# Four raw slots in the value stage, and the residual added on TensorE

## The chip, the cores and the metric

The kernel runs as one program on one core of one Trainium2 chip. The metric is the time of one launch on the device in microseconds (us). A time is the median of several launches. The profile is of one launch, and its span runs from the first to the last instruction.

## The reference, cut to what matters

The whole computation is two transformer blocks on 256 tokens of width 2048: a gated MLP and a stick-breaking attention, then a convolution with an mLSTM, and a layer of picked experts (PEER). The change lies in the last part of that layer and in the last norm. For each token 8 heads pick 16 experts each, of 16,384; each pick has a row of `u` and a row of `v`:

```
# peer_ffn, per token t, 128 picks: eid (expert), gate (softmax of the scores)
act = gelu(sum_d u[eid, d] * x[t, d])
ff[t] = sum over picks of gate * act * v[eid]          # v: (16384, 2048)
# the last lines of second_block
h = layernorm(ALPHA * h + ff, ln2_g, ln2_b)            # ALPHA = 2 ** 0.25
```

Everything is float32.

## The kernel before, in words

The 256 tokens are two tiles of 128 (`TILES = 2`), tokens on the partitions. The residual is `h`, 128 partitions x 2 tiles x 2048 columns. All the large products before the value stage run on TensorE from weights that are streamed in, rounded on ScalarE (`hi`) and completed on VectorE (`lo`), with three products for hi*hi, lo*hi and hi*lo.

The layer of experts comes in three steps. First the `u` rows are gathered, 8 KB each, by GpSimd's indirect DMAs into `ring`, and VectorE takes the dot products (L1847). Meanwhile and behind it the picks are turned into a table: for each token, one-hot matrices (VectorE, L1830 and L1834) are multiplied on TensorE (L925, `scatter`), and ScalarE stores the result as `wT` (L1215, `store_w`). `wT` holds the weight of every one of the 16,384 experts for every token, as 128 chunks of 128 experts.

Then comes the value stage, around which the change is made. It splits the 2048 columns of `v`:

- The first 1536 columns (`V_DENSE`) are done as a dense product: all 16,384 rows of `v` are streamed, in 128 chunks of 128 rows x 1536 columns (768 KB). SyncE issues the load of chunk c into `v_raw[c % 2]` (`load_v`, L476); that slot is free once VectorE has made the low part of chunk c-2 (semaphore `v_lo`). ScalarE rounds the chunk's weights (L1224, `round_w`) and then the chunk itself (L1229, `round_v`) into `v_split`, which has two slots; it waits for TensorE to have finished chunk c-2 (`v_products`). VectorE makes the low parts (`lo_v`: L1925 for the weights, L1928 for the chunk). TensorE adds 18 products of 128x128 by 128x512 per chunk into six PSUM banks, three of `half0` and three of `half1` (`multiply_v`, L941).
- The last 512 columns (`V_GATHERED`) are done by gathering: 128 picks x 2 tiles, one indirect DMA of 128 rows of 2 KB each (L574) into four slots `v_rows`, and one multiply-add on VectorE for each (`weigh`, L1911). VectorE's program alternates: one `lo_v`, two `weigh`. A gather may be issued when VectorE has used the row set four before it.

So five engines walk through 128 chunks side by side: SyncE and GpSimd issue transfers that share the 16 DMA engines, ScalarE rounds, VectorE completes and weighs, TensorE multiplies. Each engine's program is in order; the semaphores named above couple them.

Behind the last product VectorE makes `h*ALPHA + PSUM` for each tile (L1955), the statistics (L1958 and what follows), ScalarE applies scale and shift (L1262), and VectorE multiplies by the gain and adds the bias in four pieces of 1024 columns (L1970, L1971); each piece is then stored.

## Time and profile before

| | us |
|---|---|
| median of 3 runs | 3249.94 (3248.04 to 3255.05) |
| span of the profiled execution | 3249.8 |
| TensorE (PE) busy, whole span | 2416.7 (74%) |
| VectorE (DVE) busy, whole span | 2225.1 (68%) |
| ScalarE (ACT) busy, whole span | 1095.1 (34%) |
| GpSimd (POOL) busy, whole span | 824.5 (25%) |
| L941, the products of the value stage, x2304 | 548.6 busy |
| L1928, low part of a chunk of `v`, x128 | 225.0 busy |
| L1229, rounding of a chunk of `v`, x128 | 190.6 busy |
| mean granted TensorE clock, share of 2.4 GHz | 0.872 |

The page does not give the profiled execution's own launch time; its span stands 0.1 us under the median, so sums are made against 3249.8. In the timeline each row is a start time, a duration, the engine with the line and the operation, what it writes and reads, and, in brackets, how long the engine was idle before it and who ended that wait. Rows of one line that follow one another without idle time are merged, with their count behind the x. A few matmul records can be missing, so counts of merged matmuls are nearly, not always exactly, whole chunks.

### The profile page before, as it was taken

What the parts mean: (1) busy time and instruction counts of PE and PEld (TensorE: products, weight loads), DVE (VectorE), ACT (ScalarE), POOL (GpSimd) and SP (SyncE); (2) the same over time, 40 slices, a digit from 0 to 9 for tenths busy, and PEclk for the clock granted to TensorE, in tenths of its full rate; (3) what the DMA queues carried; (4) which work ended last, traced back from release to release, by engine and by line L of the source; (5) the groups of instructions that cost most, each with busy time, mean ns of one, the idle gap of its engine ahead of it and who ended that gap; (6) DMA issues with size and microseconds to landing.
All of it is one profiled execution on the core that took longest, in us unless ns stands there. A gap on an engine that the chain in (4) does not pass through costs nothing.

```text
span 3249.8 us, 32810 instructions
## 1 busy us (share of the span) xinstructions
PE 2416.7 (74%) x10945; PEld 1994.8 (61%) x10945; DVE 2225.1 (68%) x2822; ACT 1095.1 (34%) x1069; POOL 824.5 (25%) x548
## 2 busy tenths in 40 slices
PE   7999999999999998999998400001111389998996
PEld 6888888888888886888887400001111267777775
DVE  4456455555445556356656899999999987777777
ACT  4444444444445543344444100000000134343343
POOL 1000000000000000000000466676557435555553
PEclk8999999999999998899999755555555699999998
DMA  7666556556665454455564688898789548888886
GB/s 246 194 187 185 178 181 188 186 190 188 185 184 162 136 201 157 143 162 182 181 231 140 267 368 363 373 410 339 308 315 381 230 166 287 284 285 296 282 284 211
DMA packets 164690, 766.49 MB, mean 236 GB/s; under 512 B 20124, under 2 KB 20176, under 8 KB 130672
## 3 DMA queue, kind: packets, MB, share of 16 engines
q1 hardware_dynamic: 104800, 415.28, 39.9%
q0 software_dynamic: 59792, 349.90, 27.7%
q8 instruction: 62, 1.02, 0.1%
q14 instruction: 36, 0.29, 0.0%
HBM read 763.00 MB, written 2.10 MB: 235 GB/s over the span
## 4 chain that ended last, share of the span: by engine, by line
PE 54%; DVE 25%; DMA 11%; issue 6%; ACT 3%; DVEq 1%; SPq 0%; POOL 0%; POOLq 0%; ACTq 0%
PE half L600 49%; DVE ring L1847 14%; DMA v_raw<-in_peer_v 9%; DVE v_split L1928 3%; ACT v_split L1229 2%; DVE onehot_a L1834 2%; PE half L619 1%; DMA v_rows<-in_peer_v,idx 1%; DMA w_raw<-in_a_w_in 1%; DVE onehot_b L1830 1%; PE half L941 1%; PE half L796 1%; DVEq L1834 0%; PE half L668 0%; DVE left L1745 0%
## 5 line engine op out<-in xcount | busy, mean ns | idle before, releaser
L600 PE MATMUL half<-w_split,xT 128*128 128x512 f32 x7104 | 1639.4, 392 | 14.8 <-DVE xT L1296 12.2
L600 PEld LDWEIGHTS half<-w_split,xT 128*128 128x128 f32 x7104 | 1338.1, 189 | 294.4 <-issue 8.1
L1277 DVE TENSOR_TENSOR w_split<-w_raw,w_split 128x1024 fp32r<-128x1024 f32 x592 | 722.5, 1225 | 764.6 <-ACT w_split L981 763.8
L981 ACT ACTIVATE w_split<-w_raw 128x1024 fp32r<-128x1024 f32 x592 | 626.5, 1059 | 943.2 <-PE half L600 914.8
L560 POOL DMA_INDIRECT ring<-in_peer_u,idx x256 | 480.9, 1878 | 439.6 <-DVE dots L1847 186.2
L941 PE MATMUL half<-v_split,w_x 128*128 128x512 f32 x2304 | 548.6, 395 | 46.0 <-ACT v_split L1229 43.3
L1847 DVE CUSTOM_DVE_ANT_0 ring<-ring,h 128x2048 f32<-128x2048 f32 x256 | 570.0, 2285 | 5.0 <-issue 2.5
L941 PEld LDWEIGHTS half<-v_split,w_x 128*128 128x128 f32 x2304 | 428.6, 189 | 165.8 <-ACT v_split L1229 76.0
L574 POOL DMA_INDIRECT v_rows<-in_peer_v,idx x256 | 327.9, 1281 | 333.6 <-DVE v_odd L1911 209.2
L925 PE MATMUL half<-onehot_a,onehot_b 128*128 128x128 f32 x512 | 95.0, 362 | 334.8 <-DVE onehot_a L1834 334.8
L925 PEld LDWEIGHTS half<-onehot_a,onehot_b 128*128 128x128 f32 x512 | 87.9, 268 | 342.1 <-DVE onehot_a L1834 342.1
L1928 DVE TENSOR_TENSOR v_split<-v_raw,v_split 128x1536 fp32r<-128x1536 f32 x128 | 225.0, 1758 | 102.4 <-ACT v_split L1229 102.3
L1229 ACT ACTIVATE v_split<-v_raw 128x1536 fp32r<-128x1536 f32 x128 | 190.6, 1489 | 292.5 <-DMA v_raw<-in_peer_v 292.5
L498 POOL DMA_DIRECT2D row_a<-in_final_g x1 | 0.5, 531 | 1130.2 <-DVE ao L1503 1130.2
L1215 ACT ACTIVATE wT<-half 128x1024 f32 x32 | 32.8, 1024 | 395.6 <-PE half L925 395.6
L914 PE MATMUL half<-ident,wgt 128*128 128x128 f32 x2 | 0.9, 473 | 186.2 <-DVE wgt L1863 186.2
L914 PE MATMUL half<-ident,pick_keys 128*128 128x128 f32 x4 | 1.0, 353 | 184.1 <-DVE v_odd L1877 184.1
L1911 DVE SCALAR_TENSOR_TENSOR v_odd<-v_rows,wgt,v_odd 128x512 f32<-128x512 f32 x128 | 95.8, 748 | 36.2 <-DMA v_rows<-in_peer_v,idx 35.8
L914 PEld LDWEIGHTS half<-ident,wgt 128*128 128x128 f32 x2 | 0.4, 180 | 186.8 <-DVE wgt L1863 186.8
L914 PEld LDWEIGHTS half<-ident,pick_keys 128*128 128x128 f32 x4 | 0.6, 177 | 184.3 <-issue 184.3
L1911 DVE SCALAR_TENSOR_TENSOR h<-v_rows,wgt,h 128x512 f32<-128x512 f32 x128 | 95.4, 745 | 7.1 <-DMA v_rows<-in_peer_v,idx 7.1
L1196 ACT ACTIVATE gate<-gate 128x32 f32<-128x32 f32 x8 | 1.7, 225 | 264.6 <-DVE gate L1778 264.6
(287 smaller groups left out, 1201.2 us busy)
## 6 DMA issues: line engine op xcount, KB each, us to landing
w_raw<-in_a_w_in SPq DMA_DIRECT2D x192, 512.0 KB, 3.6
v_raw<-in_peer_v SPq DMA_DIRECT2D x128, 768.0 KB, 5.8
w_raw<-in_b_w_in SPq DMA_DIRECT2D x128, 512.0 KB, 3.5
w_raw<-in_w_in SPq DMA_DIRECT2D x112, 512.0 KB, 3.5
w_raw<-in_a_w_out SPq DMA_DIRECT2D x64, 512.0 KB, 3.6
w_raw<-in_b_w_out SPq DMA_DIRECT2D x32, 512.0 KB, 4.6
w_raw<-in_w_out SPq DMA_DIRECT2D x32, 512.0 KB, 4.6
w_raw<-in_peer_wq SPq DMA_DIRECT2D x32, 512.0 KB, 3.7
```

The lines of the kernel that those rows point to most:

```text
L560: nc.gpsimd.indirect_dma_start(out=ring[:, s, :], out_offset=None, in_=peer_u_2[0], in_offset=bass.IndirectOffsetOnAxis(ap=idx[:, b, s:s + ...
L574: nc.gpsimd.indirect_dma_start(out=v_rows[n % V_SLOTS][:, :], out_offset=None, in_=peer_v_2[0].rearrange("e (s d) -> (e s) d", s=V_PARTS), ...
L600: last = mm(ps[half][:, 2 * t + n, :], xt[:, xp, kk, tok], w_split[:, s, wp, n * BANK:(n + 1) * BANK], start=(k == 0 and xp == 0 and wp == ...
L925: last = mm(by_128[s][:, n, :], onehot_b[:, s, n, :], onehot_a[:, s, n, :], start=True, stop=True)
L941: ins = mm(ps[t][:, n, :], w_x[s][:, xp, 1 - t, 0, :], v_split[s][:, vp, n * BANK:(n + 1) * BANK], start=first and xp + vp == 0, stop=last ...
L981: fn(w_split[:, k % SPLIT_SLOTS, 0, :], w_raw[:, k % RAW_SLOTS, :], ACT.Copy).then_inc(hi_done, 1)
L1229: fn(v_split[s][:, 0, :], v_raw[s][:, :], ACT.Copy).then_inc(v_hi, 1)
L1277: v.tensor_tensor(w_split[:, s, 1, :], w_raw[:, k % RAW_SLOTS, :], w_split[:, s, 0, :].bitcast(F32), ALU.subtract).then_inc(split_done, 1)
L1834: ins = v.tensor_scalar(onehot_a[:, s, n, :], iota_keys[:, :], picksT[:, 0, bass.ds(token + n, 1)], picksT[:, 2, bass.ds(token + n, 1)], A ...
L1847: v.tensor_tensor_reduce(out=ring[:, s, :], in0=ring[:, s, :], in1=h[:, t, :], scale=1.0, scalar=0.0, op0=ALU.mult, op1=ALU.add, accum_out ...
L1911: v.scalar_tensor_tensor(out=acc, in0=v_rows[m % V_SLOTS][:, :], scalar=wgt[:, bass.ds(i * BODY + m, 1)], in1=acc, op0=ALU.mult, op1=ALU.a ...
L1928: v.tensor_tensor(v_split[s][:, 1, :], v_raw[s][:, :], v_split[s][:, 0, :].bitcast(F32), ALU.subtract)\
```

## The change

`v_raw` gets four slots instead of two. The two new ones lie in the memory of `h`, over its first 1536 columns (`H` for tile 0, `H + D * 4` for tile 1). For that the dense part of `h` must be gone from there: it is put into the PSUM sums before the first chunk, as the product of a scaled identity (`ident_alpha` = ALPHA on the diagonal, made by ScalarE) with `h`, six plain float32 matmuls of 128x128 by 128x512 (`seed_h`), which open the six sums. The loads into the two new slots wait for these matmuls (`h_seeded`). ScalarE's and SyncE's loops have four chunks in a body instead of two. In the last norm the multiply-add of `h` and PSUM goes; statistics and ScalarE's scale and shift read PSUM directly, ScalarE in three instructions for each tile instead of two.

```
...
@@ -211,6 +212,7 @@
         moments = tiny("moments", [P, TILES, 2])
         shift = tiny("shift", [P, TILES])
         warm = tiny("warm", [P, 1])
+        ident_alpha = sb("ident_alpha", [P, P], F32, SCR + 48 * KB)
 
 
         xg = sb("xg", [P, TILES, D], F32, SCR)
@@ -313,7 +315,8 @@
         V_CHUNK = V_DENSE * 4
         lists = packer(ROWS, LISTS)
         v_raw = [lists("v_raw0", [P, V_DENSE]),
-                 sb("v_raw1", [P, V_DENSE], F32, ROWS + 24 * KB - 288 - V_CHUNK)]
+                 sb("v_raw1", [P, V_DENSE], F32, ROWS + 24 * KB - 288 - V_CHUNK),
+                 sb("v_raw2", [P, V_DENSE], F32, H), sb("v_raw3", [P, V_DENSE], F32, H + D * 4)]
         w_x = [lists(f"w_x{n}", [P, 2, TILES, 1, P], F32R) for n in range(2)]
         v_split = [sb("v_split0", [P, 2, V_DENSE], F32R, RAW), sb("v_split1", [P, 2, V_DENSE], F32R, SCR + 32 * KB)]
         v_rows = ([sb(f"v_rows{n}", [P, V_GATHERED], F32, RAW + 2 * V_CHUNK + n * V_GATHERED * 4) for n in range(2)]
@@ -388,7 +391,9 @@
-        v_raw_landed = [sem("v_raw_landed0"), sem("v_raw_landed1")]
+        v_raw_landed = [sem(f"v_raw_landed{n}") for n in range(V_RAW_SLOTS)]
+        alpha_ready = sem("alpha_ready")
+        h_seeded = sem("h_seeded")
@@ -471,17 +476,19 @@
                 if s == 1 and isinstance(c, int):
 
                     sp.wait_ge(scattered, TOKENS // SCATTER + 2)
+                if s == 2 and isinstance(c, int):
+                    sp.wait_ge(h_seeded, 1)
                 if not isinstance(c, int):
-                    sp.wait_ge(v_lo, c - 1)
+                    sp.wait_ge(v_lo, c - (V_RAW_SLOTS - 1))
                 sp.dma_start(v_raw[s][:, :], peer_v_2[0, bass.ds(c * N_KEYS, N_KEYS), 0:V_DENSE])\
                     .then_inc(v_raw_landed[s], 16)
 
             sp.wait_ge(keys_known, TILES)
-            for s in range(2):
+            for s in range(V_RAW_SLOTS):
                 load_v(s, s)
-            with sp.Fori(1, N_KEYS // 2) as i:
-                for s in range(2):
-                    load_v(i * 2 + s, s)
+            with sp.Fori(1, N_KEYS // V_RAW_SLOTS) as i:
+                for s in range(V_RAW_SLOTS):
+                    load_v(i * V_RAW_SLOTS + s, s)
             for n in range(2 * TILES):
                 t, b = divmod(n, 2)
                 cols_ = slice(b * COLS, (b + 1) * COLS)
@@ -934,12 +941,21 @@
                 turn_picks(f"wgtT{t}", [wgt[:, t * PICKS:(t + 1) * PICKS]])
                 scatter(t)
 
-            def multiply_v(c, s, first=False, last=False):
+            def seed_h():
+
+                pe.wait_ge(alpha_ready, 1)
+                for t in range(TILES):
+                    for n in range(V_BANKS):
+                        ins = mm(ps[t][:, n, :], ident_alpha[:, :], h[:, t, n * BANK:(n + 1) * BANK], start=True,
+                                 stop=False)
+                ins.then_inc(h_seeded, 1)
+
+            def multiply_v(c, s, last=False):
 
                 def one(t, xp, vp):
                     for n in range(V_BANKS):
                         ins = mm(ps[t][:, n, :], w_x[s][:, xp, 1 - t, 0, :], v_split[s][:, vp, n * BANK:(n + 1) * BANK],
-                                 start=first and xp + vp == 0, stop=last and vp == 1)
+                                 start=False, stop=last and vp == 1)
                     return ins
 
                 pe.wait_ge(v_hi, c + 1)
@@ -956,9 +972,8 @@
 
             pe.wait_ge(w_stored, TOKENS // SCATTER + 2)
             emptied("wgtT1")()
-            multiply_v(0, 0, first=True)
-            multiply_v(1, 1)
-            with pe.Fori(1, N_KEYS // 2 - 1) as i:
+            seed_h()
+            with pe.Fori(0, N_KEYS // 2 - 1) as i:
                 for s in range(2):
                     multiply_v(i * 2 + s, s)
             multiply_v(N_KEYS - 2, 0)
@@ -1219,17 +1234,18 @@
 
             def round_w(c, s):
 
-                if not isinstance(c, int):
+                if not (isinstance(c, int) and c < 2):
                     act.wait_ge(v_products, c - 1)
-                fn(w_x[s][:, 0, :, :, :], wT[:, :, bass.ds(c, 1), :], ACT.Copy).then_inc(w_hi, 1)
+                fn(w_x[s % 2][:, 0, :, :, :], wT[:, :, bass.ds(c, 1), :], ACT.Copy).then_inc(w_hi, 1)
 
             def round_v(c, s):
 
-                act.wait_ge(v_raw_landed[s], c * 8 + (16 - 8 * s))
-                fn(v_split[s][:, 0, :], v_raw[s][:, :], ACT.Copy).then_inc(v_hi, 1)
+                act.wait_ge(v_raw_landed[s], c * (16 // V_RAW_SLOTS) + (16 - 16 // V_RAW_SLOTS * s))
+                fn(v_split[s % 2][:, 0, :], v_raw[s][:, :], ACT.Copy).then_inc(v_hi, 1)
 
             for n in range(TILE_GROUPS + 1):
                 gate_exponent(n)
+            fn(ident_alpha[:, :], ident[:, :], ACT.Copy, scale=ALPHA).then_inc(alpha_ready, 1)
             pick_gelu(0)
             picks_out("pkT0", picksT[:, 0:2, 0:P], 2)
             picks_out("wgtT0", picksT[:, 2:3, 0:P], 1)
@@ -1248,18 +1264,22 @@
             for s in range(2):
                 round_w(s, s)
             round_v(1, 1)
-            with act.Fori(1, N_KEYS // 2) as i:
-                for s in range(2):
-                    round_w(i * 2 + s, s)
-                    round_v(i * 2 + s, s)
+            for s in range(2, V_RAW_SLOTS):
+                round_w(s, s)
+                round_v(s, s)
+            with act.Fori(1, N_KEYS // V_RAW_SLOTS) as i:
+                for s in range(V_RAW_SLOTS):
+                    round_w(i * V_RAW_SLOTS + s, s)
+                    round_v(i * V_RAW_SLOTS + s, s)
 
             warm_root()
             for t in range(TILES):
                 root_next(slice(t, t + 1))
                 act.wait_ge(shift_ready, t + 1)
-                for b in range(2):
-                    cut = h[:, t, b * COLS:(b + 1) * COLS]
-                    fn(cut, cut, ACT.Identity, bias=shift[:, t:t + 1], scale=rstd[:, t:t + 1]).then_inc(normed, 1)
+                affine = dict(bias=shift[:, t:t + 1], scale=rstd[:, t:t + 1])
+                fn(h[:, t, 0:COLS], flat[t][:, 0:COLS], ACT.Identity, **affine).then_inc(normed, 1)
+                fn(h[:, t, COLS:V_DENSE], flat[t][:, COLS:V_DENSE], ACT.Identity, **affine)
+                fn(h[:, t, V_DENSE:], h[:, t, V_DENSE:], ACT.Identity, **affine).then_inc(normed, 1)
 
 
         @block.vector
@@ -1919,13 +1939,16 @@
                 dve.wait_ge(v_used, (t + 1) * PICKS + V_SLOTS)
                 step(v.tensor_tensor(h[:, t, V_DENSE:], h[:, t, V_DENSE:], v_odd[:, :], ALU.add))
 
-            def lo_v(c, s):
+            def lo_v(c, n):
+
+                s = n % 2
 
                 dve.wait_ge(w_hi, c + 1)
                 v.tensor_tensor(w_x[s][:, 1, :, :, :], wT[:, :, bass.ds(c, 1), :], w_x[s][:, 0, :, :, :].bitcast(F32),
                                 ALU.subtract).then_inc(w_lo, 1)
                 dve.wait_ge(v_hi, c + 1)
-                v.tensor_tensor(v_split[s][:, 1, :], v_raw[s][:, :], v_split[s][:, 0, :].bitcast(F32), ALU.subtract)\
+                v.tensor_tensor(v_split[s][:, 1, :], v_raw[n % V_RAW_SLOTS][:, :], v_split[s][:, 0, :].bitcast(F32),
+                                ALU.subtract)\
                     .then_inc(v_lo, 1)
 
             with dve.Fori(0, P // SCATTER // 2) as i:
@@ -1951,11 +1974,8 @@
                 v.bn_stats(bn[:, t, V_BANKS, :], h[:, t, V_DENSE:])
             dve.wait_ge(v_products, N_KEYS)
             for t in range(TILES):
-                dst = h[:, t, 0:V_DENSE]
-                step(v.scalar_tensor_tensor(out=dst, in0=dst, scalar=ALPHA, in1=flat[t][:, 0:V_DENSE], op0=ALU.mult,
-                                            op1=ALU.add))
                 for n in range(V_BANKS):
-                    ins = v.bn_stats(bn[:, t, n, :], h[:, t, n * BANK:(n + 1) * BANK])
+                    ins = v.bn_stats(bn[:, t, n, :], flat[t][:, n * BANK:(n + 1) * BANK])
                 step(ins)
                 step(tile_moments(t))
                 v.tensor_scalar(meansq[:, t:t + 1], moments[:, t, 1:2], LN_EPS, None, ALU.add).then_inc(stat, 1)
```

SyncE's program at the start of the value stage, before (`v_raw_155` and `v_raw_156` are the two slots; a row in brackets names the semaphores waited for):

```order
L476 DMA v_raw_155<-in_peer_v 128x1536 [waits keys_known]
L476 DMA v_raw_156<-in_peer_v 128x1536 [waits scattered]
L482 UNCONDITIONAL_BRANCH
L482 ISA
L476 ISA [waits v_lo]
L476 DMA v_raw_155<-in_peer_v 128x1536
L476 ISA [waits v_lo]
L476 DMA v_raw_156<-in_peer_v 128x1536
```

and after (four slots, `v_raw_156` to `v_raw_159`):

```order
L483 DMA v_raw_156<-in_peer_v 128x1536 [waits keys_known]
L483 DMA v_raw_157<-in_peer_v 128x1536 [waits scattered]
L483 DMA v_raw_158<-in_peer_v 128x1536 [waits h_seeded]
L483 DMA v_raw_159<-in_peer_v 128x1536
L489 UNCONDITIONAL_BRANCH
L489 ISA
L483 ISA [waits v_lo]
L483 DMA v_raw_156<-in_peer_v 128x1536
L482 REGISTER_ALU
L483 ISA [waits v_lo]
L483 DMA v_raw_157<-in_peer_v 128x1536
L482 REGISTER_ALU
```

The load of chunk 2 moved from behind the first `v_lo` to behind `h_seeded`, and each later load waits for the low part of four chunks before.

TensorE's program between the last one-hot product and the second group of products of the first chunk, before:

```order
L925 MATMUL half<-onehot_a,onehot_b 128x128 [waits w_stored,onehot_done]
L925 MATMUL half<-onehot_a,onehot_b 128x128 x7
L919 REGISTER_ALU
L919 COMPARE_AND_BRANCH
L941 MATMUL half<-v_split_159,w_x_157 128x512 [waits v_hi,w_hi,half_free_a,w_stored]
L941 MATMUL half<-v_split_159,w_x_157 128x512 x5
L941 MATMUL half<-v_split_159,w_x_157 128x512 [waits w_lo]
```

and after (L949 is `seed_h`):

```order
L932 MATMUL half<-onehot_a,onehot_b 128x128 [waits w_stored,onehot_done]
L932 MATMUL half<-onehot_a,onehot_b 128x128 x7
L926 REGISTER_ALU
L926 COMPARE_AND_BRANCH
L949 MATMUL half<-h,ident_alpha 128x512 [waits alpha_ready,half_free_a,w_stored]
L949 MATMUL half<-h,ident_alpha 128x512 x5
L976 UNCONDITIONAL_BRANCH
L976 ISA
L957 MATMUL half<-v_split_162,w_x_160 128x512 [waits w_hi,v_hi]
L957 MATMUL half<-v_split_162,w_x_160 128x512 x5
L957 MATMUL half<-v_split_162,w_x_160 128x512 [waits w_lo]
```

Six matmuls stand ahead of the first chunk, and the first chunk's products are now in the loop.

VectorE's program behind the last row set (`half` is PSUM), before:

```order
L1920 TENSOR_TENSOR h<-h,v_odd 128x512 [waits v_used]
L1951 BN_STATS bn<-h 128x6 [waits dve_step]
L1951 BN_STATS bn<-h 128x6
L1955 SCALAR_TENSOR_TENSOR h<-h,half 128x1536 [waits v_products]
L1958 BN_STATS bn<-h 128x6 [waits dve_step]
L1958 BN_STATS bn<-h 128x6 x2
L1335 BN_AGGR moments<-bn 128x2 [waits dve_step]
L1961 TENSOR_SCALAR meansq<-moments 128x1 [waits dve_step]
L1317 RECIPROCAL rstd<-root 128x1 [waits rooted]
L1963 SCALAR_TENSOR_TENSOR shift<-moments,rstd 128x1 [waits dve_step]
L1955 SCALAR_TENSOR_TENSOR h<-h,half 128x1536
L1958 BN_STATS bn<-h 128x6 [waits dve_step]
```

and after:

```order
L1940 TENSOR_TENSOR h<-h,v_odd 128x512 [waits v_used]
L1974 BN_STATS bn<-h 128x6 [waits dve_step]
L1974 BN_STATS bn<-h 128x6
L1978 BN_STATS bn<-half 128x6 [waits v_products]
L1978 BN_STATS bn<-half 128x6 x2
L1355 BN_AGGR moments<-bn 128x2 [waits dve_step]
L1981 TENSOR_SCALAR meansq<-moments 128x1 [waits dve_step]
L1337 RECIPROCAL rstd<-root 128x1 [waits rooted]
L1983 SCALAR_TENSOR_TENSOR shift<-moments,rstd 128x1 [waits dve_step]
L1978 BN_STATS bn<-half 128x6 x3
```

L1955 is gone for both tiles, and the statistics read `half`; the rows behind them are unchanged.

## Rows read from the trace of the kernel before

**Rows 1.** The page's chain of waits over the whole span, shares by engine and line.
```profile
PE 54%; DVE 25%; DMA 11%; issue 6%; ACT 3%; DVEq 1%; SPq 0%; POOL 0%; POOLq 0%; ACTq 0%
```

**Rows 2.** The chain of waits from 2550 us on, shares by line.
```profile
by line: DMA v_raw<-in_peer_v 43.3%; DVE v_split L1928 12.9%; ACT v_split L1229 10.7%; issue 8.4%; DMA v_rows<-in_peer_v,idx 5.7%; DVE onehot_a L1834 3.8%; PE half L941 2.6%; DVE ring L1847 2.6%; DVE h L1911 1.2%; DVEq L1834 1.0%; PE half L
```

**Rows 3.** TensorE's timeline in the value stage: first run, a long one, longest idle, last.
```profile
2634.16 12.58 PE L941 MATMUL half<-v_split,w_x 128*128 128x512 f32 x54 [1.75 <-ACT w_x L1224]
...
2688.81 20.72 PE L941 MATMUL half<-v_split,w_x 128*128 128x512 f32 x90 [0.40 <-ACT v_split L1229]
...
2932.17 22.30 PE L941 MATMUL half<-v_split,w_x 128*128 128x512 f32 x90 [4.80 <-ACT v_split L1229]
...
3200.60 26.45 PE L941 MATMUL half<-v_split,w_x 128*128 128x512 f32 x108 [1.90 <-ACT v_split L1229]
```

**Rows 4.** Waits from 2600 us on: who waited for whom; total us, times, longest.
```profile
ACT v_split L1229 <- DMA v_raw<-in_peer_v: 292.5, 125, 7.3
POOL v_rows L574 <- DVE v_odd L1911: 209.2, 93, 71.7
...
DVE v_odd L1911 <- DMA v_rows<-in_peer_v,idx: 35.8, 44, 1.9
```

**Rows 5.** The instructions on tile v_raw: durations ns min/median/max, then landing.
```profile
L1229 ACT ACTIVATE v_split<-v_raw x128: 1471/1490/1497, 2577.8 to 3221.1; 128x1536 fp32r<-128x1536 f32 x128
L1928 DVE TENSOR_TENSOR v_split<-v_raw,v_split x128: 1748/1758/1809, 2634.5 to 3222.7; 128x1536 fp32r<-128x1536 f32 x128
...
DMA to landing us min/median/max: 4.0/5.8/10.2
```

**Rows 6.** DMA queues, 2640 to 3220 us: packets, MB, share of the 16 engines; issues.
```profile
q1 hardware_dynamic: 18002, 98.29, 50.6%
q0 software_dynamic: 20322, 67.79, 33.0%
...
row_b<-in_ln_b POOLq DMA_DIRECT2D x1, 1024.0 KB, 11.8
```

**Rows 7.** Windows: us, busy (count) of PE, PEld, DVE, ACT, POOL, PEclk, DMA share, GB/s.
```profile
2600.00:2634.00 34.00, 21.05 (x165) 18.95 (x164) 30.30 (x88) 11.66 (x13) 0.00 (x0) 1.00 0.01 2
2640.00:3220.00 580.00, 535.72 (x2250) 418.42 (x2249) 434.16 (x534) 231.88 (x250) 319.64 (x253) 0.99 0.84 286
```

**Rows 8.** Timeline of one gather's round, and landings of all v_rows gathers.
```profile
2961.14 0.74 DVE L1911 SCALAR_TENSOR_TENSOR v_odd<-v_rows,wgt,v_odd 128x512 f32<-128x512 f32 x1
...
2963.35 1.91 POOL L574 DMA_INDIRECT v_rows<-in_peer_v,idx  x1 [0.31 <-issue]
...
2970.72 0.75 DVE L1911 SCALAR_TENSOR_TENSOR v_odd<-v_rows,wgt,v_odd 128x512 f32<-128x512 f32 x1 [1.09 <-DMA v_rows<-in_peer_v,idx]
...
DMA to landing us min/median/max: 3.4/5.2/11.7
```

**Rows 9.** Timeline: VectorE from one chunk to the next without a wait.
```profile
2654.94 0.42 DVE L1925 TENSOR_TENSOR w_x<-wT,w_x 128x256 fp32r<-128x256 f32 x1
...
2658.27 0.42 DVE L1925 TENSOR_TENSOR w_x<-wT,w_x 128x256 fp32r<-128x256 f32 x1
```

**Rows 10.** Timeline at the stage's start; float32 matmuls of 256 columns by form.
```profile
2632.55 1.02 ACT L1215 ACTIVATE wT<-half 128x1024 f32 x1 [2.17 <-PE half L925]
...
L668 PE MATMUL half<-gv,wsT 128*128 128x256 f32 x64 | 14.5, 379 | 0.0
```

**Rows 11.** Timeline of the last norm.
```profile
3227.70 1.74 DVE L1955 SCALAR_TENSOR_TENSOR h<-h,half 128x1536 f32<-128x1536 f32 x1
3229.47 1.88 DVE L1958 BATCH_NORM_STATS2 bn<-h 128x6 f32<-128x512 f32 x3
...
3237.08 1.23 DVE L1970 TENSOR_TENSOR h<-h,row_g 128x1024 f32<-128x1024 f32 x1
3237.19 2.37 ACT L1262 ACTIVATE h<-h,shift,rstd 128x1024 f32<-128x1024 f32 x2 [0.42 <-DVE shift L1963]
```

More of the change, by code:

```diff
@@ L71 @@
 V_SLOTS = 4
+V_RAW_SLOTS = 4
 SCATTER = 8
@@ L1938, in stream_v @@
                     for n in range(BODY // 2):
-                        lo_v(i * (BODY // 2) + (t * (N_KEYS // TILES) + n), n % 2)
+                        lo_v(i * (BODY // 2) + (t * (N_KEYS // TILES) + n), n)
                         weigh(t, i, t * PICKS + 2 * n)
```

## The prediction

> **What bounds the kernel now.** I read the page's chain of waits first, since it says which engine the end hangs on: 54% of the span is TensorE [rows 1], nearly all of it in stages that the change does not touch. The same chain cut to the last 700 us reads quite otherwise: the transfer of a raw chunk leads with 43.3%, VectorE's low part has 12.9%, ScalarE's rounding 10.7%, and the products only 2.6% [rows 2]. So the value stage is not bound by TensorE, though TensorE looks full in it.
>
> TensorE's timeline gives the stage's size. It runs from 2634.16 to 3200.60 + 26.45 = 3227.05, which is 592.9 us for 128 chunks, 4.63 us per chunk. Where it is fed it does five chunks in 20.72 us, less the 0.16 us by which the last record outlasts its issue (estimate: a record lasts 0.39, the next starts after 0.23), so 4.11 us per chunk; I use 4.12 [rows 3]. All 128 at this rate take 527.4 us, so 65.5 us of the stage are gaps, each ended by ScalarE's rounding of a chunk. The waits say what ScalarE stood for: 292.5 us in 125 waits for the transfer of a raw chunk [rows 4].
>
> The reason is a loop with two slots. A load is issued at the end of the low part of two chunks before; it lands after 5.8 us (median), is rounded in 1.49 and gets its low part in 1.76 [rows 5]. That is 9.05 us for two chunks, 4.53 each, and with some 0.2 us of hand-overs 4.63, the measured pace. So the loop, not an engine, sets it. The other bounds, per chunk:
>
> - TensorE 4.12.
> - DMA engines: 83.6% of 580 us busy, 485 us for 125 chunks, 3.88 us [rows 6]. Their rate is 286 GB/s at a share of 0.84 [rows 7], so some 340 if full; at 4.12 us per chunk the share would be 0.94.
> - VectorE 3.33 where it does not wait: from 2654.94 to 2658.27 [rows 9].
> - The gathers' loop, with four slots, so two chunks for a round: multiply-add 0.74, then 1.47 until the gather is issued (2961.88 to 2963.35, the one ahead of it in GpSimd's queue included), then the wait for the rows. Here the rows were used 7.37 us after the issue, and VectorE waited for them: a round of 9.58, 4.79 per chunk. With the median landing of 5.2 the round is 7.4, 3.7 per chunk [rows 8]. With L for the latency, the pace is (2.21 + L) / 2. GpSimd itself has room: it waits 209.2 us for VectorE to free a slot [rows 4].
>
> **The change part by part.** *Four raw slots.* The load of chunk c+4 is issued at the low part of chunk c. The loop of 9.26 us is now shared by four chunks, 2.3 us each, far below 4.12. The stall of raw chunks goes, and TensorE is next at 4.12, with the gathers between 3.7 and 4.8 close beside it. VectorE now waits for gathers 35.8 us in 44 waits, 0.8 us each [rows 4]. It has 4.12 - 3.33 = 0.79 us to spare per chunk, and its low part may come late, since only the last third of a chunk's products waits for it; most single waits are swallowed. But the DMA engines go from 0.84 to above 0.9, and L with them; TensorE keeps pace only while L stays under 2 x 4.12 - 2.21 = 6.03, and the landings spread from 3.4 to 11.7. Bounds for the stage: 527.4 us if nothing reaches TensorE, and (2.21 + 7.37) / 2 x 128 = 613 us if every gather were as late as the one shown. I take 545, nearer the first, since L's median of 5.2 is well under 6.03: 527.4, plus 15 us (0.12 per chunk) for late gathers, plus 3 of the present 4.8 us gap before 2932.17 [rows 3], where two 1 MB rows stand ahead of gathers in GpSimd's queue (11.8 us to land [rows 6]); slots of raw chunks bridge only the dense half of this. Gain 47.9 us. All loads keep their number and size, and SyncE passes only waits for the low part, so nothing is queued behind a later wait than before.
>
> By the Trainium skill, "DMA: Bandwidth & Descriptors", section "Queues, rings and completion order", each DMA engine takes turns between the queues with work, one packet each. No row shows a standing backlog, because two slots can't build one.
>
> *Residual first, through the identity.* Six float32 matmuls of 512 columns are new at the stage's start. The nearest rows are float32 matmuls of 256 columns, two records for each, 64 records in 14.5 us, 0.227 a record [rows 10]. At twice the width 0.44 to 0.45, so 12 x 0.44 = 5.3 us; bounds 12 x 0.23 = 2.8 (as cheap as the stage's own products) and 10.6 (half clock; but the clock is 1.00 from 2600 to 2634 [rows 7]). They start when the last table part is stored, 2632.55 + 1.02 = 2633.57 [rows 10], while the first product now starts at 2634.16, after ScalarE's rounding, which now runs beside them. Cost 5.3 - 0.6 = 4.7 us, all on the path, since TensorE is what the stage waits for. The loads of chunks 2 and 3 wait for this: issued at 2638.9 instead of 2636.3. They land by 2644.7, are rounded by 2646.3, and TensorE wants chunk 2 at 2638.9 + 8.2 = 2647.1; covered by 0.8 us, and if the load takes as long as the 10.2 us maximum it costs 3.6 us once. Scaling the identity is one short ScalarE instruction long before, hidden by VectorE's picks; uncovered it would cost under its 1.02 us row for eight times the columns. The first low part and its gathers are not behind the seeds and may run ahead.
>
> *Last norm.* Two multiply-adds of 1.74 go from VectorE's path, 3.5 us; VectorE is never idle for long from 3227.70 to the end [rows 11]. They also started 0.65 us after the last product, since VectorE had the last row set to finish; with TensorE the pacer it should be done sooner, and I count 0.6 us. The six statistics read PSUM. L1955 read PSUM and took 1.74 [rows 11], where L1928 took 1.758 on as many columns of SBUF [rows 5]: no surcharge, cost nothing; the bound on the other side is 1 us in all (estimate: 10% of 2 x 1.88, rounded up for hand-overs). ScalarE's third instruction for each tile adds some 0.2 us; VectorE's eight passes of 1.23 start at 3237.08 while ScalarE's two for the same tile took 2.37 together, so it is covered; if not, 0.4 us. In all -4.1.
>
> The Trainium skill, "VectorE: DVE Perf Modes", section "The TRN2 errata", gives VectorE a fixed 120 cycles with a PSUM source against 58 with SBUF. By it the six statistics would lose 6 x 65 ns = 0.4 us; the rows above do not bear it out.
>
> Sum: 3249.8 - 47.9 + 4.7 - 4.1 = 3202.5 us. The median is 0.1 above the span, so **3203 us**.
>
> **The rivals.**
>
> A, *TensorE alone paces.* Late gathers are all swallowed: 527.4 for the stage, 3249.8 - 65.5 + 0.6 = 3185 us. For it: at 2688.81 five chunks ran with no gap even now. Against it: five runs on a stretch need not hold for 128, and the 4.8 us gap has a cause that stays.
>
> B, *gathers take the place of the raw loads.* Mean L of 6.7, midway between the median and the late ones: 4.45 per chunk, 570 us, -23 + 0.6, so 3227 us. For it: VectorE is already made to wait by the second gather of a chunk 44 times, and the load on the DMA engines grows. Against it: the issue pattern per chunk stays, one raw load and two gathers, so the two compete hardly more often than now. The packet rule of the Trainium skill above is a milder version of this; estimated by it, 3249.8 - 36 + 0.6 = 3214 us.
>
> C, *the slots bring nothing.* If the long landing of raw chunks is the DMA engines' own limit, more slots only lengthen the landing, and the pace stays at 4.6: 3250 us. Against it: the engines are busy 0.84, and the shortest landing is 4.0 us.
>
> D, *slower.* With up to four raw loads queued, gathers land late in every round. The point from which it decides is L = 2 x 4.63 - 2.21 = 7.05; beyond it the stage is longer than now. At L = 7.5, just over the late one shown, the pace is 4.86, the stage 622 us, and the whole 3249.8 + 29 + 0.6 = 3279 us. For it: 7.37 was seen. Against it: it would have to be the mean.
>
> **How the numbers follow.** Forecast 0.55 (its own range 3192 to 3214), A 0.15, B 0.20, C 0.04, D 0.06. No change means within 0.2% (6.5 us) of the median, about what a measurement can tell here; so faster 0.90, same 0.04, slower 0.06. The range reaches down to A and up past B: 3184 to 3232.
>
> **What would show it.** In the profile after: ScalarE's wait for raw chunks falls from 292.5 us to a few tens, and its rounding waits for TensorE's products instead; TensorE's gaps in the stage fall from 65 us to about 18, ended by low parts (VectorE) rather than by rounding; DMA share 0.9 or more at some 308 GB/s; twelve records near 0.44 us ahead of the first chunk; VectorE's statistics within 0.7 us of the last product, at 0.63 us each. The forecast fails if VectorE's waits for gathers grow beyond 100 us with a pace over 4.4 (B or D), or if raw chunks still end ScalarE's waits (C).

## The result

| | before | after |
|---|---|---|
| median, us | 3250.27 (8 runs) | 3233.53 (8 runs) |
| span of the profiled execution, us | 3249.8 | 3230.0 |
| ratio of the times | | 0.995, 95% interval 0.9939 to 0.9961 |

The kernel became faster by 0.5%, some 17 us, where 47 us were forecast; the measured time lies just above the range that was given (3232). The profiled execution is 19.8 us shorter than that of before, and the following speaks of these two. (The forecast took a median to stand 0.1 us above a profiled span. Here the profiled launch took 3232.14 us for a span of 3230.0, and the median stands 1.4 us above that, so the two can't be compared to a microsecond.) The value stage runs from 2636.96 to 3208.84, 571.9 us, 4.47 us per chunk instead of 4.63. So of the 19.8 us the stage gave 21.0; its first product came 2.8 us later, and what follows the last product was 1.5 us shorter.

TensorE's timeline after, the seeds, the first run of chunks, a run of five chunks, the two gaps beside the gain rows and the last run; the brackets tell the idle time and who ended it:

```profile
2632.11 5.42 PE L949 MATMUL half<-h,ident_alpha 128*128 128x512 f32 x12 [1.21 <-ACT wT L1230]
...
2636.96 51.61 PE L957 MATMUL half<-v_split,w_x 128*128 128x512 f32 x222
...
2716.28 21.55 PE L957 MATMUL half<-v_split,w_x 128*128 128x512 f32 x90 [0.52 <-DVE w_x L1947]
...
2922.96 4.72 PE L957 MATMUL half<-v_split,w_x 128*128 128x512 f32 x18 [2.08 <-DVE w_x L1947]
2929.85 8.80 PE L957 MATMUL half<-v_split,w_x 128*128 128x512 f32 x36 [2.17 <-DVE w_x L1947]
...
3193.28 15.56 PE L957 MATMUL half<-v_split,w_x 128*128 128x512 f32 x66 [0.52 <-DVE w_x L1947]
```

Against [rows 3] the reader sees another releaser: not ScalarE's rounding but VectorE's low part of the weights. The first 222 products go in 51.61 us, 0.232 each; VectorE starts ahead, and it takes some twelve chunks until its lateness has reached TensorE. Later 90 products take 21.55 us, where 90 took 20.72 in [rows 3]: part of the time is lost in pauses of a few tenths inside a merged run, between the three groups of a chunk. So the pace must be taken from duration and count together, not from the idle time shown in brackets.

Who waited for whom after 2640 us, after; total us, times, longest:

```profile
DVE v_odd L1931 <- DMA v_rows<-in_peer_v,idx: 123.3, 117, 2.4
...
PEld half L957 <- DVE w_x L1947: 33.1, 51, 2.6
PEld half L957 <- DVE v_split L1950: 32.2, 84, 0.5
```

and the same view from 2600 us on has one more row of interest:

```profile
ACT v_split L1244 <- DMA v_raw<-in_peer_v: 2.5, 1, 2.5
```

ScalarE's 292.5 us of waits for raw chunks [rows 4] are 2.5. VectorE's waits for the second gather of a chunk grew from 35.8 us in 44 to 123.3 in 117: nearly every chunk. The chain of waits says the same; its shares from 2640 to 3200 us, after:

```profile
by line: DMA v_rows<-in_peer_v,idx 56.1%; issue 15.6%; POOL v_rows L581 13.2%; DVE v_odd L1931 5.5%; PE half L957 4.2%; DVE v_split L1950 1.5%; DVE h L1931 0.8%; DMA v_raw<-in_peer_v 0.8%; POOLq L579 0.5%; DVEq L1931 0.5%; DVE w_x L1947 0.4
```

In [rows 2], over a longer stretch, the raw transfer led with 43.3% and the gathers had 5.7%; over the same 560 us of the trace before they have 54.2% and 6.3%. The landings of all gathers, after, against a median of 5.2 in [rows 8]:

```profile
DMA to landing us min/median/max: 3.4/6.4/11.8
```

Three rounds of second gathers in the timeline after; VectorE's use of a row set, GpSimd's gather into its slot, and the use of what it brought:

```profile
2646.66 0.75 DVE L1931 SCALAR_TENSOR_TENSOR v_odd<-v_rows,wgt,v_odd 128x512 f32<-128x512 f32 x1 [0.58 <-DMA v_rows<-in_peer_v,idx]
...
2648.53 1.70 POOL L581 DMA_INDIRECT v_rows<-in_peer_v,idx  x1 [0.30 <-issue]
...
2650.21 0.75 DVE L1931 SCALAR_TENSOR_TENSOR v_odd<-v_rows,wgt,v_odd 128x512 f32<-128x512 f32 x1
...
2652.10 2.26 POOL L581 DMA_INDIRECT v_rows<-in_peer_v,idx  x1 [0.30 <-issue]
...
2655.96 0.75 DVE L1931 SCALAR_TENSOR_TENSOR v_odd<-v_rows,wgt,v_odd 128x512 f32<-128x512 f32 x1 [1.57 <-DMA v_rows<-in_peer_v,idx]
...
2657.49 2.05 POOL L581 DMA_INDIRECT v_rows<-in_peer_v,idx  x1 [1.38 <-DVE v_odd L1931]
...
2660.07 0.80 DVE L1931 SCALAR_TENSOR_TENSOR v_odd<-v_rows,wgt,v_odd 128x512 f32<-128x512 f32 x1 [0.69 <-DMA v_rows<-in_peer_v,idx]
...
2664.40 0.75 DVE L1931 SCALAR_TENSOR_TENSOR v_odd<-v_rows,wgt,v_odd 128x512 f32<-128x512 f32 x1 [0.86 <-DMA v_rows<-in_peer_v,idx]
```

The gather issued at 2648.53 is used at 2655.96, after 7.43 us; that of 2652.10 after 7.97; that of 2657.49 after 6.91. The round from 2646.66 to 2655.96 is 9.30 us, the next of the same slots, 2655.96 to 2664.40, is 8.44: in the mean 8.87 for two chunks, 4.44 each, close to the stage's 4.47. Over all second gathers of this trace, the landing comes 7.0 us after the issue in the median; in the trace before, where only half of them (63) can be told, 5.3. That 5.3 is the middle of two groups. When GpSimd's issue of the gather took under 1.2 us, the rows landed 4.6 us after it in the mean (33 gathers); when it took 1.9 or more, 6.9 (18 gathers). And the 44 second gathers for which VectorE already waited before were used 7.1 us after their issue in the mean; after the change there are 117 such, and they were used 7.2 us after. So the late gathers did not become later, nearly all became late: the changed kernel is paced by a round that stood just under the bound before.

The windows of the two traces over the same 500 us, before and then after (columns as in [rows 7]):

```profile
2640.00:3140.00 500.00, 461.95 (x1941) 359.63 (x1940) 374.72 (x461) 199.99 (x216) 274.96 (x219) 1.00 0.84 287
```

```profile
2640.00:3140.00 500.00, 486.01 (x2014) 368.14 (x2013) 381.52 (x472) 201.28 (x224) 328.08 (x224) 1.00 0.84 298
```

The DMA engines' share stayed at 0.84, and they moved 11 GB/s more. That they were not full is shown below, by e6. GpSimd is busy 53 us longer for as good as the same number of gathers.

The tail after, from the last row set to VectorE's first pass over the normed tiles:

```profile
3208.64 0.75 DVE L1931 SCALAR_TENSOR_TENSOR v_odd<-v_rows,wgt,v_odd 128x512 f32<-128x512 f32 x1 [2.42 <-DMA v_rows<-in_peer_v,idx]
...
3211.36 1.88 DVE L1978 BATCH_NORM_STATS2 bn<-half 128x6 f32<-128x512 f32 x3
...
3214.38 1.20 ACT L1280 ACTIVATE h<-half,shift,rstd 128x1024 f32<-128x1024 f32 x1 [0.43 <-DVE shift L1983]
...
3217.35 1.22 DVE L1990 TENSOR_TENSOR h<-h,row_g 128x1024 f32<-128x1024 f32 x1
```

The three statistics from PSUM take 1.88 us, exactly what they took from SBUF [rows 11]. But VectorE reaches them 2.5 us after the last product (3208.84), because the last gather was late as well.

### The profile page after: what moved, and what is told of

Read it like the earlier page. It is cut to its first block, busy times and chain, and to the rows that moved or that the text cites. A ratio compares the mean times of both kernels' runs of the same rounds, so it can differ in the third digit from the quotient of the medians.

```text
span 3230.0 us, 32701 instructions
## 1 busy us (share of the span) xinstructions
PE 2428.1 (75%) x10957; PEld 1987.9 (62%) x10957; DVE 2219.0 (69%) x2820; ACT 1088.4 (34%) x1072; POOL 877.8 (27%) x548
## 4 chain that ended last, share of the span: by engine, by line
PE 54%; DVE 23%; DMA 11%; issue 7%; POOL 2%; ACT 1%; DVEq 1%; POOLq 0%; SPq 0%; ACTq 0%
PE half L607 49%; DVE ring L1867 14%; DMA v_rows<-in_peer_v,idx 10%; POOL v_rows L581 2%; DVE onehot_a L1854 2%; PE half L626 1%; DVE v_odd L1931 1%; PE half L957 1%; DMA w_raw<-in_a_w_in 1%; DVE onehot_b L1850 1%; PE half L803 1%; DVEq L1854 0%; PE half L675 0%; DVE left L1765 0%; PE half L906 0%
## 5 line engine op out<-in xcount | busy, mean ns | idle before, releaser
L957 PE MATMUL half<-v_split,w_x 128*128 128x512 f32 x2304 | 557.0, 397 | 14.9 <-DVE w_x L1947 13.9
L957 PEld LDWEIGHTS half<-v_split,w_x 128*128 128x128 f32 x2304 | 421.5, 188 | 150.2 <-DVE w_x L1947 33.1
L581 POOL DMA_INDIRECT v_rows<-in_peer_v,idx x256 | 381.3, 1489 | 267.0 <-DVE v_odd L1931 159.4
L1931 DVE SCALAR_TENSOR_TENSOR v_odd<-v_rows,wgt,v_odd 128x512 f32<-128x512 f32 x128 | 96.5, 754 | 123.4 <-DMA v_rows<-in_peer_v,idx 123.3
L1239 ACT ACTIVATE w_x<-wT 128x256 fp32r (+1 forms) x128 | 53.5, 419 | 339.1 <-PE half L957 339.1
```

The lines of the kernel that those rows point to most:

```text
L581: nc.gpsimd.indirect_dma_start(out=v_rows[n % V_SLOTS][:, :], out_offset=None, in_=peer_v_2[0].rearrange("e (s d) -> (e s) d", s=V_PARTS), ...
L957: ins = mm(ps[t][:, n, :], w_x[s][:, xp, 1 - t, 0, :], v_split[s][:, vp, n * BANK:(n + 1) * BANK], start=False, stop=last and vp == 1)
L1931: v.scalar_tensor_tensor(out=acc, in0=v_rows[m % V_SLOTS][:, :], scalar=wgt[:, bass.ds(i * BODY + m, 1)], in1=acc, op0=ALU.mult, op1=ALU.a ...
```

## The experiments

Theory G, formed from the two traces: two rounds bound the stage side by side, and each spans as many transfers as it has slots. Before, the raw loads' round of two slots gave 4.63 us per chunk; after, the second gather's round of four slots (two chunks) gives 4.47. Rivals: the DMA engines have no more to give; the gain came from the seeds and the norm; VectorE's own work is the bound; the loops' register work delays gathers. Times are medians of four to ten runs (two for e2), with the ratio to the kernel before and its 95% interval; each ratio goes by runs of the kernel before taken together with the version's own, so it can differ a little from that of the medians shown. The pace is that of TensorE's stage in one traced execution. It was the fastest run of its version in e3 and e8 and the slowest in e4 (of 3199 to 3222 us), e7 and e10.

| version | median us | ratio (interval) | us per chunk |
|---|---|---|---|
| before | 3250.27 | 1 | 4.63 |
| changed | 3233.53 | 0.995 (0.9939 to 0.9961) | 4.47 |
| e1, two raw slots | 3249.78 | 0.9993 (0.9983 to 1.0003) | 4.61 |
| e2, half raw loads | 3182.95 | 0.9788 (0.9769 to 0.9808) | 4.09 |
| e3, multiply-add between | 3225.94 | 0.9922 (0.9906 to 0.9939) | 4.42 |
| e4, slots four and two | 3210.46 | 0.9861 (0.984 to 0.9881) | 4.40 |
| e5, raw loads later | 3223.16 | 0.9917 (0.9894 to 0.994) | 4.44 |
| e6, six row slots in turn | 3180.0 | 0.9786 (0.9769 to 0.9802) | 4.10 |
| e7, gain rows last | 3230.91 | 0.9936 (0.9919 to 0.9952) | 4.48 |
| e8, three raw loads ahead | 3228.52 | 0.9934 (0.9918 to 0.9951) | 4.45 |
| e9, e6 with two raw slots | 3244.43 | 0.9976 (0.9966 to 0.9986) | 4.55 |
| e10, e6 with four row slots | 3227.26 | 0.9914 (0.9898 to 0.9931) | 4.45 |
| e11, e6 with gain rows last | 3181.41 | 0.9778 (0.9761 to 0.9794) | 4.08 |

**e1: the slots undone, the rest kept.**

```
-V_RAW_SLOTS = 4
+V_RAW_SLOTS = 2
```

> The changed kernel with the raw slots back at two; the residual still goes in through the identity and the last norm still reads PSUM. Theory G (the gathers' round now paces the changed kernel at 4.47 us per chunk, and the two-slot loop of raw loads did so before at 4.63): the pace goes back to 4.63, the stage to about 593 us, so about 21 us slower than the changed kernel, near 3254 us, and TensorE's 5.0 us of seeds and the 4 us of the last norm about cancel against the kernel before. Rival (the gain came from the seeds and the norm, not from the slots): it stays near 3233 us.

The pace went back to 4.61, and against the kernel before nothing measurable is left. So the whole gain is the slots', and the seeds and the norm cancel. In its trace TensorE's stage ends 16.3 us before the end of VectorE's last pass, against 19.7 before; this stretch is called the tail in what follows.

**e2: half of the raw traffic.**

```
-sp.dma_start(v_raw[s][:, :], peer_v_2[0, bass.ds(c * N_KEYS, N_KEYS), 0:V_DENSE])\
+wide = V_DENSE if isinstance(c, int) else V_DENSE // 2
+sp.dma_start(v_raw[s][:, 0:wide], peer_v_2[0, bass.ds(c * N_KEYS, N_KEYS), 0:wide])\
     .then_inc(v_raw_landed[s], 16)
```

> The changed kernel, but each raw load after the first four brings only the first 768 of its 1536 columns; the rest of a slot is stale, so the dense part is not the reference's. All engines' work is the same, the raw traffic on the DMA engines is halved. Theory G with contention on the DMA engines as the reason for late gathers: the second gather of a chunk lands 7.0 us after its issue in the changed kernel; here under 6 us, and TensorE paces at 4.12 to 4.2 (stage 528 to 538 us). If it is GpSimd's longer issue (1.9 us instead of 0.95 beside VectorE's low part) that makes it late, the issue stays at 1.9 us, the landing near 6.5, and the pace about 4.25.

TensorE paces at 4.09, and VectorE's waits for gathers fall to 8.6 us:

```profile
DVE v_odd L1932 <- DMA v_rows<-in_peer_v,idx: 8.6, 21, 1.0
```

GpSimd's issue of second gathers stayed as long as in the changed kernel, 1.97 us in the mean against 1.89, so that alone does not make them late. What shrank is the time from the end of the issue to VectorE's use, from 5.3 to 4.1 us in the mean. The raw traffic beside them makes it long, with four row slots and everything else equal. Were it the issue alone, a pace of about 4.25 was forecast; it did not come.

**e3: the two multiply-adds apart.** `lo_v` calls the first `weigh` of the chunk between its two low parts.

```
-def lo_v(c, n):
+def lo_v(c, n, between):
...                                       # low part of the weights
+between()
 dve.wait_ge(v_hi, c + 1)
...                                       # low part of the chunk
-lo_v(i * (BODY // 2) + (t * (N_KEYS // TILES) + n), n)
-weigh(t, i, t * PICKS + 2 * n)
+lo_v(i * (BODY // 2) + (t * (N_KEYS // TILES) + n), n,
+     lambda: weigh(t, i, t * PICKS + 2 * n))
 weigh(t, i, t * PICKS + 2 * n + 1)
```

> The changed kernel with VectorE's order in a chunk changed: low part of the weights, first multiply-add, low part of the chunk, second multiply-add. The two slots of a chunk come free 1.8 us apart or more instead of 0.66, so the second gather is not queued behind the first in GpSimd's program or on the DMA engines. Theory G: its round shrinks from 8.94 us to about 8.2, the pace to 4.15, 35 to 40 us faster than the changed kernel, near 3195 us. Rival (VectorE's lateness, not the gathers, holds TensorE): the low part of the chunk comes 0.75 us later than now and the kernel gets no faster or a few us slower.

Faster than the changed kernel by some 8 us, not 35 to 40: a miss of G's size. Now the first gather is the late one:

```profile
DVE h L1931 <- DMA v_rows<-in_peer_v,idx: 108.5, 106, 4.2
...
DVE v_odd L1931 <- DMA v_rows<-in_peer_v,idx: 13.3, 10, 2.1
```

The lateness moved with the order. Whatever gather is issued while VectorE makes the 1.75 us low part takes GpSimd longer: in the changed kernel the issue of second gathers took 1.94 us in the mean when it overlapped that work (120 of them) and 0.94 when not, that of first gathers 1.08; here first gathers take 1.58 and second ones 1.12.

**e4: four slots for the second gather, two for the first.**

```
+ROW_SLOT = [0, 1, 2, 3, 0, 4, 2, 5]      # by pick % 8; slots 4 and 5 lie behind v_split1
...
+for m in range(BODY, 2 * BODY, 2):       # the second gather of a chunk, two chunks further ahead
+    gather_row(i, m)
+    gather_row(i, m + 5)
...
```

> The changed kernel with six slots for gathered rows instead of four: the second gather of each chunk has four slots and is issued four chunks ahead, the first keeps two. Theory G: the second gather's round spans four chunks and no longer binds, the first one's is 0.75 + 0.8 + 5.5 = 7.1 us for two chunks; TensorE paces at 4.12 to 4.2, near 3195 us, and VectorE's 129 us of waits for gathers nearly go. Rival (the DMA engines give no more than 296 GB/s in this mix of rows and chunks): landings get longer in turn, the pace stays near 4.45, 3230 us.

Half of it came true. The second gather never waits, but the first, still two chunks ahead, now makes VectorE wait 121.7 us in 71 waits. Its round had been hidden behind the other's. The times lie between the forecast and the rival's 3230, from 3199 to 3222 us.

**e5: raw loads 1.4 us later.**

```
-sp.wait_ge(v_lo, c - (V_RAW_SLOTS - 1))
+sp.wait_ge(v_used, c * 2 - 2)
```

> The changed kernel, with each raw load issued when VectorE has used both row sets of the chunk four before (v_used) instead of at that chunk's low part: 1.4 us later against the gathers, same depth. Raw chunks land 5.3 us before ScalarE takes them (median in the changed kernel), so they can wait. Theory P (the second gather is late because the next raw load, issued at a fixed phase, runs beside it): its landing falls from 7.0 by 0.5 to 1 us, the pace to 4.2 to 4.35, 3205 to 3220 us. Rival B (the two transfers share the DMA engines wherever the load stands, since they are 83% busy): unchanged within 5 us, 3233.

Between the two forecasts, and with runs from 3210 to 3249 us the least steady of all. The waits split, 63.6 us for second and 54.3 us for first gathers, 118 together against 129: the phase moves the lateness more than it removes it.

**e6: six row slots in turn.** GpSimd's and VectorE's loops of the stage are written out, since 16 picks a body do not go into six slots.

```
-V_SLOTS = 4
+V_SLOTS = 6
...
+                  + [sb(f"v_rows{n}", [P, V_GATHERED], F32, SCR + 44 * KB + (n - 4) * V_GATHERED * 4) for n in (4, 5)])
...                                       # GpSimd, the slot being m % V_SLOTS
+for m in range(TILES * PICKS):
...
+    if m == 4:
+        pool.wait_ge(scattered, TOKENS // SCATTER + 2)
+    pool.wait_ge(v_used, m + 1)
...
```

> The changed kernel with six slots for gathered rows used in turn, so every gather is issued three chunks ahead of its use instead of two (GpSimd's and VectorE's loops of the value stage are written out for it). Theory G: the round of some 8.9 us now spans three chunks, 3.0 us each, and nothing of it reaches TensorE but the two gain rows: 4.12 to 4.2 per chunk, 3193 to 3203 us, and VectorE's waits for gathers under 20 us. With four and two slots (the run before) the first gather, still two chunks ahead, was the late one: 121.7 us in 71 waits. Rival (DMA engines full): pace 4.4, 3225 us.

It is 70 us faster than the kernel before and 53 faster than the changed one. TensorE's stage is two merged rows with one gap:

```profile
2635.00 267.17 PE L957 MATMUL half<-v_split,w_x 128*128 128x512 f32 x1176
2902.88 256.30 PE L957 MATMUL half<-v_split,w_x 128*128 128x512 f32 x1128 [0.71 <-DVE w_x L1947]
```

That is 524.2 us for 128 chunks, 4.095 each. The window of the same 500 us:

```profile
2640.00:3140.00 500.00, 499.29 (x2202) 412.83 (x2201) 420.68 (x522) 220.43 (x246) 394.52 (x245) 1.00 0.92 326
```

The DMA engines give 326 GB/s at a share of 0.92 where the changed kernel stood at 298 and 0.84. This rules out that they were full. VectorE's own work is not the bound either: it is busy 420.68 of these 500 us, while TensorE is busy all but 0.71. With TensorE last, VectorE starts the statistics at once and the tail is 15.7 us, against 19.7 before: the 4 us that were forecast.

**e7: gain rows last.**

```
-    if t == 0:
-        pool.wait_ge(v_products, D // P)
-        row(row_g2[:, :], ln2_g_2[0], "rows_ln2")
-        row(row_b2[:, :], ln2_b_2[0], "rows_ln2")
+pool.wait_ge(v_products, D // P)          # behind both tiles' gathers
+row(row_g2[:, :], ln2_g_2[0], "rows_ln2")
+row(row_b2[:, :], ln2_b_2[0], "rows_ln2")
```

> The changed kernel with the two 1 MB rows of gain and bias loaded behind the last gather instead of between the tiles. In the changed kernel TensorE loses some 4 us at 2921 and 2928 beside them. Theory G: 3 to 6 us faster, near 3229 us, since gathers pace all the stage and those two loads stand in their queue. Rival: the loads then end too late for the last norm (needed 14 us after the last gather) and it is 0 to 5 us slower.

2.6 us faster in the median, with overlapping runs (3229.12 to 3234.86 against 3231.48 to 3237.91); the trace, which is of the slowest of the four runs, shows none of it (4.48 per chunk). Inconclusive.

**e8: one raw load less ahead.**

```
-sp.wait_ge(v_lo, c - (V_RAW_SLOTS - 1))
+sp.wait_ge(v_lo, c - (V_RAW_SLOTS - 2))
```

> The changed kernel with each raw load held until the low part of the chunk three before, so one of the four slots is always empty: same phase against the gathers, one load less ahead. Theory P: nothing changes, 3233 us within 4, since raw chunks now land 5.3 us early and would still land 1 us early. If a standing backlog of raw loads is what makes gathers late, the second gather's landing falls under 6.5 us and the kernel gets 10 to 25 us faster.

5 us faster, at the edge of what was allowed for "nothing"; VectorE waited 118.9 us for second gathers instead of 123.3, and still used them 7.2 us after their issue in the mean. The fourth load ahead, which was to bring 10 to 25 us if it mattered, is not what makes gathers late. The run says less of the raw traffic itself: in the changed kernel a raw load is issued once per chunk, every 4.47 us, and lands 6.2 us later (median), so some 1.4 are under way in the mean, and holding one slot back leaves that rate as it is.

**e9 and e10: controls for e6.**

```
-V_RAW_SLOTS = 4                      # e9
+V_RAW_SLOTS = 2
-V_SLOTS = 6                          # e10, otherwise written out as e6
+V_SLOTS = 4
```

> Six row slots used in turn as in the fast version, but two raw slots as before the change. Theory G says that the two rounds are separate bounds, and the slower one sets the pace: the raw loads' round of two slots again gives about 4.6 us per chunk, 3245 to 3252 us, although gathers no longer make VectorE wait. Rival (row slots alone would have brought the gain, the raw slots nothing): 3180 to 3200 us.

> The fast version with four row slots instead of six, GpSimd's and VectorE's loops of the value stage still written out: a control for the writing out. Theory G: as the changed kernel, 3233 us within 5, second gathers late again. Rival (the loops' register work and branches were what delayed gathers): near 3180 us.

Both as G says. With six row slots and two raw slots ScalarE waits for raw chunks again:

```profile
ACT v_split L1244 <- DMA v_raw<-in_peer_v: 259.0, 122, 5.5
```

and with four row slots VectorE waits for gathers again, written out or not:

```profile
DVE v_odd L1929 <- DMA v_rows<-in_peer_v,idx: 122.2, 112, 2.5
```

Four raw slots alone are worth 17 us. Six row slots, with the loops written out, are worth 5 us with two raw slots (e9 against e1) and 53 with four (e6 against the changed kernel): each deepening alone runs into the other round. Writing out alone is worth some 6 us by the medians and 12 by the ratios (e10 against the changed kernel), so the loops' instructions did cost something, and why is not shown; the row slots themselves are worth 47 of the 53 us by the medians (e6 against e10), and in e9 nothing that can be told from the writing out.

**e11: e6 with gain rows last.** Moved as in e7.

> The version with six row slots, and the rows of gain and bias loaded behind the last gather. With six slots TensorE has one gap of 0.7 us in the whole stage, so there is at most that to win; the loads land about 12 us after the last gather's issue at 3147.7, at about 3161, and the norm wants them at about 3167. Theory G: the same time within 2 us, 3180.

The same time, as expected. e6 stays the fastest version that was run, with e11 beside it.

## Why the prediction was wrong, step by step

- *The raw loads' round bounds the kernel.* Right. e1 goes back to 4.61, and the wait for raw chunks fell from 292.5 to 2.5 us with four slots. Its removal was said to leave a round of 2.3 us per chunk; the raw chunks did land 5.0 us before ScalarE took them, in the median of all 128.
- *TensorE is next at 4.12.* Right as a bound, 4.08 to 4.10 in e2, e6 and e11, but it was not next.
- *Late gathers cost 15 us, 0.12 per chunk.* This is the step that failed. The stage took 571.9 us, 44.5 more than the 527.4 of TensorE alone, where 18 were allowed (15, and 3 beside the gain rows). The prediction named the condition itself: TensorE keeps pace while the latency stays under 6.03 us. It took the median landing of all gathers, 5.2 [rows 8], for the mean round, while its own example of a waiting gather had 7.37. That first and second gathers were mixed in that median did no harm (5.2 and 5.3 before); that it was a middle between early and late ones did. The 44 second gathers that made VectorE wait had 7.1 from issue to use even before, and in the changed kernel 117 of the last 126 did, with 7.2. With (2.21 + L) / 2, L = 7.2 gives 4.7. The measured 4.47 is less, mainly because the issue came 1.04 us after the slot was free in the mean, not 1.47: (0.75 + 1.04 + 7.23) / 2 = 4.51, which is VectorE's pace over the stage, and VectorE had started ahead of TensorE.
- *The issue pattern stays, so the transfers compete hardly more often.* Wrong. This was the argument against rival B. When VectorE no longer waits for ScalarE, the low part follows the second multiply-add sooner (0.3 us behind its end in the mean, 1.2 before); the second gather's issue falls beside it and is stretched (1.43 us before, 1.89 after, in the mean), and the next raw load comes closer behind the start of that issue (1.4 us instead of 1.95). The trace before has this pattern in part of its chunks, with the same effect: of the second gathers whose landing can be told, those with the next raw load issued within 1.6 us landed after 6.9 us in the mean (20), the others after 5.0 (42). Moving the raw load's phase (e5) or taking one load ahead less (e8) brings back only 5 to 10 us; e2 shows that with half the raw bytes all of it is gone. Of the 1.7 us of longer landing (in medians), 0.9 lie behind the end of the issue (4.3 before, 5.2 after); the rest lies in the issue. What each would cost without the other no run tells.
- *B, gathers take the place of the raw loads*: 4.45 us per chunk, 570 us, 3227. This is what happened, 4.47, 571.9, span 3230.0, though its L of 6.7 was too small and its delay until the issue too large, and the two errors nearly cancelled. It had a chance of 0.20 and should have had the most. The range ended at 3232, just short of the measured 3233.53.
- *The packet rule* (the Trainium skill, "DMA: Bandwidth & Descriptors", section "Queues, rings and completion order") pointed the right way, by an estimate 557 us for the stage. But raw loads did not pile up: some 1.4 were under way in the mean (6.2 us to land, one every 4.47), where it was 1.25 before (5.8 in 4.63), and one load ahead less (e8) left the gathers as late. Whether taking turns by packets is how raw traffic delays a gather no run here shows.
- *A and C*: with all raw bytes kept, TensorE did not pace alone until the row slots were six; that the slots bring nothing is refuted by e1, and that the DMA engines were at their limit by e6. *D* did not come: the mean time from issue to use, 7.2, was even beyond the point from which it was to decide (7.05), but the shorter delay until the issue left the round under 9.26.
- *The seeds cost 4.7 us.* The twelve records took 5.42 us to the end of the last one, 0.43 from one to the next, and TensorE's first product came at 2636.96, 4.3 us later than ScalarE's rounding of the weights would have allowed. About right, as was that the loads of chunks 2 and 3 come in time.
- *The norm saves 4.1 us.* The work went as forecast (three statistics took 1.88 us from PSUM as from SBUF), but the tail is only 1.5 us shorter in the changed kernel (18.2 against 19.7), since VectorE was 2.5 us late for it. Where TensorE paces, it is 4.0 us shorter (15.7, e2, e6 and e11).

## What to carry to other kernels

When a stage is paced by a round through a few slots, write down every other round of the same stage with its own slots and its latency where it was waited for, not the median over all transfers: here 7.1 us against 5.2, both in the trace before. Deepen the rounds that lie close to the target together: here two changes worth 17 and 5 us alone were worth 70 together (the 5 and the 70 with the loops written out). And a wait of 0.8 us that is swallowed today is a warning: here, removing the large wait next to it brought the engines closer in phase, and 44 such waits became 117.

## What the runs showed of the hardware

GpSimd's indirect DMA of 128 rows of 2 KB took 0.94 us to issue whenever VectorE was not at its 1.75 us subtraction of two SBUF operands meanwhile (90 gathers of the changed kernel, 0.94 to 0.95 us). Where the two overlapped by 1.2 us or more it never took under 2.0 us (81 gathers, 2.1 in the mean), and a short overlap cost little (in e11, 115 gathers with under 0.3 us of it took 1.07). It is the same in e2 (2.1 us in 82 gathers) and, with the roles of first and second gather exchanged, in e3 (first gathers 1.64 in 116 with overlap, 0.94 in 10 without). The raw traffic is not involved, since e2 has half of it and the same issue time. The trace does not tell why.

A second gather landed 4.6 us after its issue in the mean or 6.9, in one and the same trace (before): 4.6 with an issue of under 1.2 us (33 gathers), 6.9 with one of 1.9 or more (18). In the second case the next raw load also followed more closely, 1.5 us behind the start of the issue instead of 2.5, and no run tells the two apart.

The DMA engines went to a share of 0.92 and 326 GB/s with a mix of raw chunks and gathered rows, and all engines' waits for it came to under 8 us from 2640 us on (e6).
